# Other SBUF offsets for the weight buffers and the operands of the dense products

## The reference

```
x = first_block(x, ...)        # RWKV-7 branch and sparse attention on one input projection
x = second_block(x, mem, ...)  # gated mixer of three branches, then a convolutional feed-forward

def _mixer(...):
    proj = rmsnorm(x) @ w_in                       # 1024 x 9216
    y_a = (gb * causal_conv3(gc * v)) @ w_a_out
    y_b = silu(layernorm(causal_conv31(u * sigmoid(ug)) + bias)) @ w_b_out
    y_c = attention(q, memn @ w_kv) @ w_att_out    # 256 memory tokens, 4 heads
    return (g0 * y_a + g1 * y_b + g2 * y_c) @ w_o

def _conv_ffn(...):
    u = causal_conv3(rmsnorm(x) @ w_up)            # 1024 x 5632
    gt, up = split(u)
    return (silu(gt) * up) @ w_down                # 2816 x 1024
```

## Time and profile before

| | |
|---|---|
| three runs | 1462.99, 1462.32, 1467.27 us (median 1462.99) |
| the profiled execution | span 1458.8 us, first to last instruction; mean granted TensorE clock 0.983 |
| TensorE matmul busy | 1410.6 us, 97%, 7612 instructions |
| VectorE / ScalarE / GpSimd busy | 928.9 / 495.1 / 493.1 us |
| chain that ended last | TensorE 84%, VectorE 11%, ScalarE 3% |
| HBM read | 121.84 MB, 85 GB/s over the span |

### The profile page before, as it was taken

The page is one execution under the profiler, slowest core; times in us unless marked ns, Lnnn a source line. Parts: engine busy times, 40 slices in busy tenths (PEclk is TensorE's granted clock), DMA queues, the critical chain, the costliest instruction groups (busy, mean ns, idle before and its releaser), DMA issues.

```text
span 1458.8 us, 18647 instructions
## 1 busy us (share of the span) xinstructions
PE 1410.6 (97%) x7612; PEld 1142.5 (78%) x7612; DVE 928.9 (64%) x1327; ACT 495.1 (34%) x679; POOL 493.1 (34%) x139
## 2 busy tenths in 40 slices
PE   7999988899998999999999999999998999999998
PEld 6778646678797877888888887878886888888886
DVE  6679977435414355869969974761458888884122
ACT  5443476344324332222222223322234333332121
POOL 0004120113535322344344343334433333433441
PEclk9999999899999999999999999999999999999998
DMA  6221000203323212222322322222222222232221
GB/s 207 87 87 58 30 2 1 87 32 116 116 87 118 85 58 87 87 87 87 116 87 90 113 87 87 86 88 87 93 82 87 87 102 100 87 110 85 89 92 58
DMA packets 21349, 125.14 MB, mean 86 GB/s; under 512 B 2384, under 2 KB 3408, under 8 KB 7696
## 3 DMA queue, kind: packets, MB, share of 16 engines
q1 hardware_dynamic: 20752, 121.71, 23.6%
q10 hardware_dynamic: 512, 2.23, 0.4%
HBM read 121.84 MB, written 2.10 MB: 85 GB/s over the span
## 4 chain that ended last, share of the span: by engine, by line
PE 84%; DVE 11%; ACT 3%; issue 2%; DMA 0%; DVEq 0%; SPq 0%; ACTq 0%
PE bank L410 24%; PE bank L412 23%; PE bank L411 23%; DVE score L1988 2%; DVE misc L1987 2%; PE bank L361 1%; PE bank L1028 1%; PE bank L1044 1%; DVE conv_b L2489 1%; ACT prob L1463 1%; PE bank L679 1%; PE bank L401 1%; PE bank L896 1%; PE bank L977 1%; PE bank L634 0%
## 5 line engine op out<-in xcount | busy, mean ns | idle before, releaser
L1239 POOL TENSOR_TENSOR w_lo<-w_raw,w_hi 128x2048 fp32r<-128x2048 f32 (+1 forms) x102 | 468.6, 4594 | 755.2 <-ACT w_hi L1303 739.2
L410 PE MATMUL bank<-op_hi,w_hi 128*128 128x512 f32 x1312 | 517.2, 394 | 9.3 <-issue 6.5
L412 PE MATMUL bank<-op_hi,w_lo 128*128 128x512 f32 x1312 | 513.4, 391 | 0.0
L411 PE MATMUL bank<-op_lo,w_hi 128*128 128x512 f32 x1312 | 513.0, 391 | 0.0
L410 PEld LDWEIGHTS bank<-op_hi,w_hi 128*128 128x128 f32 x1312 | 247.3, 188 | 65.7 <-issue 9.7
L1303 ACT ACTIVATE w_hi<-w_raw 128x2048 fp32r<-128x2048 f32 (+2 forms) x109 | 205.7, 1887 | 269.2 <-PE bank L412 269.2
L411 PEld LDWEIGHTS bank<-op_lo,w_hi 128*128 128x128 f32 x1312 | 247.4, 189 | 52.9 <-issue 0.7
L412 PEld LDWEIGHTS bank<-op_hi,w_lo 128*128 128x128 f32 x1312 | 247.0, 188 | 53.1
L2382 DVE SCALAR_TENSOR_TENSOR bank<-pad_b,par,bank 128x512 f32<-128x512 f32 x232 | 175.3, 756 | 7.8
L2279 DVE TENSOR_TENSOR x_res<-bank,x_res 128x512 f32<-128x512 f32 x24 | 16.5, 691 | 132.8 <-PE bank L412 132.8
L2559 DVE TENSOR_TENSOR tmp<-tmp,conv_f 128x512 f32<-128x512 f32 x22 | 88.5, 4022 | 13.3 <-ACT tmp L1759 13.3
(11 more groups left out here) (394 smaller groups left out, 1782.4 us busy)
## 6 DMA issues: line engine op xcount, KB each, us to landing
w_raw<-in_w_units SPq DMA_DIRECT2D x104, 1024.0 KB, 4.8
w_raw<-in_w_units SPq DMA_DIRECT2D x4, 768.0 KB, 4.1
x_res<-in_x SPq DMA_DIRECT2D x8, 256.0 KB, 6.3
x_res<-in_x ACTq DMA_DIRECT2D x2, 1024.0 KB, 6.5
out<-x_res SPq DMA_DIRECT2D x8, 256.0 KB, 2.2
w_raw<-in_w_units SPq DMA_DIRECT2D x3, 512.0 KB, 8.2
w_raw<-in_w_units SPq DMA_DIRECT2D x4, 256.0 KB, 5.6
mem_tok<-in_mem SPq DMA_DIRECT2D x1, 1024.0 KB, 5.0
```

The costliest lines, as they stand in the source:

```text
L410: nc.tensor.matmul(b[:, 0:width], h, xh[:, x0 + k, 0:width], start=start and k == ks[0], stop=False)
L411: nc.tensor.matmul(b[:, 0:width], h, xl(x0 + k, width), start=False, stop=False)
L412: mm = nc.tensor.matmul(b[:, 0:width], l, xh[:, x0 + k, 0:width], start=False, stop=stop and k == ks[-1])
L1239: nc.gpsimd.tensor_tensor(w_lo[u % 2][:, 0:nk, :], w_raw[u % 2][:, 0:nk, :], w_hi[u % 2][:, 0:nk, :].bitcast(F32), ALU.subtract).then_inc( ...
```

## The change

The reserved scratch goes from its default of 16384 bytes to 1024. The base is rounded up to 2048 bytes. `at` now adds 256 bytes for each whole 8192 below offset 49152, and 2048 from there on. The four buffers of split weights get 32, 64, 128 and 256 bytes more, and R0 moves to 66 x 2048 + 96. The added bytes count in the argument `offset`, so that `w_hi1` lies at base + 24640 + 768 and `w_lo1` at base + 41216 + 1280. No instruction, shape, order or wait is changed.

```
+ROW = 2048
+SLOTS_END = 49152
...
-        base = -(-nc.sbuf_base // 32) * 32
+        base = -(-nc.sbuf_base // ROW) * ROW
 
         def at(name, offset, shape, dt=F32):
-            return nc.alloc_sbuf_tensor_at(name, [P] + shape, dt, offset=base + offset)
+            return nc.alloc_sbuf_tensor_at(name, [P] + shape, dt, offset=base + offset + (ROW if offset >= SLOTS_END else 256 * (offset // 8192)))
...
         w_raw = [at(f"w_raw{s}", 8192 * s, [CH, 256]) for s in range(2)]
-        w_hi = [at(f"w_hi{s}", 16384 + 8192 * s, [CH, 256], F32R) for s in range(2)]
-        w_lo = [at(f"w_lo{s}", 32768 + 8192 * s, [CH, 256], F32R) for s in range(2)]
+        w_hi = [at(f"w_hi{s}", 16384 + 8192 * s + (32, 64)[s], [CH, 256], F32R) for s in range(2)]
+        w_lo = [at(f"w_lo{s}", 32768 + 8192 * s + (128, 256)[s], [CH, 256], F32R) for s in range(2)]
...
-        R0 = 133504
+        R0 = 66 * ROW + 96
...
-    nc = bacc.Bacc("TRN2", target_bir_lowering=False, num_devices=1)
+    nc = bacc.Bacc("TRN2", target_bir_lowering=False, num_devices=1, dynamic_dma_scratch_size=1024)
```

## The result

The changed kernel takes 1477.33 us (median of 17 runs, 1468.42 to 1479.34), the kernel before 1465.59 (17 runs, 1460.82 to 1467.63). The ratio is 1.0072, 95% interval 1.0057 to 1.0087: 0.7% slower, 8 to 13 us. The profiled execution took 1469.61 us with a span of 1467.9, 9.1 more than the 1458.8 of before; four of the 17 runs, the profiled one among them, had a granted clock of 0.987 to 0.989 and took 1468.4 to 1469.6 us, while the other thirteen had 0.980 to 0.984 and took 1473.1 to 1479.3 (median 1477.95). The profiled execution of before had 0.983, so the 9.1 us between the two spans is less than the change costs at one clock.

The account below looks back on a forecast made before the run. TensorE's start-to-start interval in dense matmuls, set by operand-to-loaded-weights distance, was taken as the bound. Steps summed to +9.5 us, times 0.92 gave +8.8 on 1462.99: 1472 us, own range 1466 to 1478, wider range 1435 to 1490.

Parts of the forecast that it names:

- Op, even units: Op-operand matmuls with even buffers: loads of lo weights at distance 384 cost +3.2 us, of hi weights at 480 +1.6 us.
- Op, odd units: Op-operand matmuls with odd buffers: loads of hi weights at distance 192 cost +7.7 us, of lo weights at 0 nothing.
- R0 operands: 1432 matmuls on R0 tiles: even units -1.5 and -1.1 us, odd units nothing for hi and -0.4 us for lo.
- The 256-column matmuls: 384 matmuls at 118.5 ns, near the load's own 109: no change, at most -3.6 us.
- The 0.92: Share of the dense matmul steps that reaches the time, 1021 us of chain over 1113 us run: +9.5 becomes +8.8 us.
- A: Rival, chance 0.12: streams collide only near distance 0 or multiples of 128, new distances clean at 216 ns; -41 us, 1422.
- B: Rival, chance 0.17: only short distances, up to 96 bytes, are clean; -15 us, 1448.
- the lower bound: For distances that no profile row shows, a dense matmul takes at least 216 ns.
- C: Rival, chance 0.13: any distance but 0 costs the full 6.3 ns; +16 us, 1479.
- D: Rival, chance 0.07: the operand's own remainder counts, 0 being bad; +19.5 us, 1482.
- E: Rival, chance 0.12: nothing depends on these bytes in the mean; 1463.
- F: Rival, chance 0.05: new starts cost by themselves, all distances but 0 at 240 ns; +43 us, 1506.

Follow-up runs that it names:

- the shifted: Distances of the kernel before, all tiles 128 bytes lower, on the changed kernel's base and scratch with 512-byte spacers between weight slots: 1460.41 us in one run.
- the one-line version: Kernel before with only R0 changed, from 133504 to 133632, so R0 operands lie at 128 modulo 512 like the rest: 1455.85 us, ratio 0.9936.
- the scans: Blocks of 24 matmuls added after the last product of the kernel with all distances 0, varying distance, widths and formats: 1874.26 us (first), 1618.11 us (second).
- the map: Step per distance from the first of the two added-block runs, 0 to 496 bytes in steps of 16; that run took 1874.26 us.
- all the same: Changed kernel's base and scratch, 512-byte spacers, weights, op and R0 operands all at remainder 0: 1460.08 us, ratio to before 0.9958.

## Why the prediction was right

Forecast 1472 and 0.6% slower; measured 0.72% (0.57 to 0.87). Of the 5.3 us by which the median lies higher, 2.6 come from the kernel before, whose median is 1465.6 over 17 runs and was 1463.0 over the three that I added to.

- TensorE's interval sets the time, and it hangs on a distance: right, shown by the shifted and by the one-line version.
- That the forecast met the time is in part luck. For single lines of `tile` its terms are up to 7 ns off, in both directions, and the errors cancel in good part, as follows.
- Op, even units, forecast +4.8 us: 1536 x 4.4 ns = +6.8. The lo term was over (+2.9 ns for the matmul that loads lo weights, forecast 6.3); the hi term was mis-sized: "a quarter of the way to 384", 1.6 ns, measured +7.6 and +2.7 in the two that load hi weights. Even units were to come near 229 ns and came at 231.3. The straight line from 0 to 128 does not exist; 480 costs 233.3 by itself.
- Op, odd units, forecast +7.7 us: 1824 x 4.9 = +8.9. Again right in the sum and not in its parts: the hi term, 6.3, measured +2.4 and +5.4, and "distance 0, nothing" was +6.8 ns on 608 matmuls. A cheap distance is cheap only beside others like it. The prediction's own sign, that even and odd units differ, is all but absent in the means (231.3 and 231.9 ns); it is the split by line that differs.
- R0 operands, forecast -3.0 us: even units -3.8 ns (forecast -3.7), odd -1.0 (-0.5), by op2's rows. The sum is right. Its parts are not (even, by line: -6.5, -3.1, -1.7, where -3.2, -4.7, -3.2 were forecast), and half the matmuls were put to each parity, where nine of the twelve op2 units are even.
- The 256-column matmuls, forecast nothing: 117 to 125 ns after, by buffer and line, and 118 to 125 before. Right. The 109 in the term of at most -3.6 us is my estimate of a load's time, from the one-column matmuls of rows 9, whose loads start every 111.5 ns in the trace of before.
- The sum, forecast +9.5 us of steps: +12.9. The 0.92 to the time: the measured 10.5 us (0.72% of 1465.6) are 0.82 of it. The thirteen runs at 0.980 to 0.984 have a median 12.4 us above the kernel before, 0.96 of it. So the factor is good to no more than that.
- Rivals A and B needed an interval near 216 somewhere. None of the 32 distances has it, so the case on the other side is closed for 512 columns. No run shows the 216 of their terms, and of the lower bound, for a float32r matmul of 512 columns: it was read from float32 passes over 256. The plain blocks of the scans took 226.7 to 240 ns, with the operand read with step 0 218.5, and bf16 215.8. C asked for +6.3 at every distance but 0 and would have held had the rows been equal (233.3 at 32, 192, 224); its time, 1479, lies nearer to the median than 1472 does, its change, +16 us, further from the measured 8 to 13 than +8.8. So the time alone does not part the two; the map does. D is out (all the same), E is out; F asked for 240 ns, which no stretch of the changed kernel averages.
- That no offset frees the matmuls was right, 226.7 ns at the best distance, for a reason that stays open. My estimate for it, that the operand stream meets the load once in each load (one lap of 512 bytes), was wrong in its main claim: the price does not follow the length of the load (233.6, 231 and 232.4 ns at distance 32 with 128, 64 and 32 columns).

For bf16 the distance changed nothing, 215.8 ns at 0 and 32; for float32r it moved the step between 226.7 and 240 ns.

What stays open: which resource it is. The runs show its period (256 bytes), that most of the price goes when the operand's address stands still, that a shorter load does not lower the price in proportion, and that one distance can have two steps. A mixed sequence can't be priced from the map.

## What to carry to other kernels

Put the weights and the operands of float32r matmuls with 128 columns of weights and 512 of operand at the same start modulo 256 bytes, all of them; here it took 6 ns off three matmuls in ten and 0.6% off the kernel, for one number. Offsets that set buffers apart cost 2 to 8 ns a matmul in the scan at multiples of 16 bytes (240 bytes once nothing, once 10), and 4 to 5 ns in the changed kernel. For narrower forms this is no rule: with 256 operand columns distance 0 took 119.7 ns and 32 bytes 117.6, and with 64 columns of weights it took 230.0 and 64 bytes 228.2. Look at starts in the timeline, not at durations, and at which tiles a dear interval has: the trace of the kernel before already held both prices.

## What was not expected of the hardware

- A float32r matmul of 512 columns takes 226.7 ns at best, a bf16 one in the same loop 215.8, and the float32r one 218.5 when its operand is read with step 0.
- Distances that are no multiple of 16 bytes reach 240.0 ns (20 and 36 bytes).
- The same distances came at two steps, each kept through its block or unit: 240 bytes took 226.7 ns in one block (single steps 226 to 227) and 236.7 in another (234 to 240), an odd op unit of the changed kernel 231.3 in one place (226 to 236) and 233.4 in another (229 to 236). That what ran before decides which is likely and not shown.
